# Other PSUM banks for the first tiles of projections, and four moved steps, in a two-block fp32 transformer kernel

## What is computed

```python
# first block
h = rms_norm(x, mix_norm_g); fq, fk, fv, flog, dq, dk, dv = split(h @ w_in)
fox_out  = 8 heads of 64: softmax(q k / 8 + cumulated log forget gates, causal) v
diff_out = 4 heads: rms_norm((softmax(q1 k1 / 8 + alibi) - lam softmax(q2 k2 / 8 + alibi)) v) * (1 - lam_init)
x = x + concat(fox_out, diff_out) @ w_out
h = rms_norm(x, ffn_norm_g); x = x + (silu(h @ w_gate) * (h @ w_up)) @ w_down      # 2816 hidden
x = rms_norm(x, final_norm_g)
# second block
z = rms_norm(x, norm1_g) @ w_in_2 + b_in; q, k, v, c_a, c_b, g_a, g_b = split(z)
br_a = neighbourhood_attention(q, k, v, rpb) @ w_na_out                            # 8 heads
u = depthwise_conv31(c_a * sigmoid(c_b)); br_b = silu(layernorm(u)) @ w_conv_out
x = x + (sigmoid(g_a) * br_a + sigmoid(g_b) * br_b) @ w_out_2
x = x + (gelu(gate) * val) @ w_down_2, (gate, val) = depthwise_conv3(rms_norm(x) @ w_up_2)
return rms_norm(x, norm_f_g)
```

## Time and profile before

| | us |
|---|---|
| median of the runs | 1381.23 |
| lowest and highest | 1380.28, 1381.60 |
| the profiled execution | 1382.35 |
| its span, first to last instruction | 1380.5 |
| TensorE busy in it | 1339.8 |
| VectorE, ScalarE, GpSimd busy | 676.5, 634.0, 665.6 |

### The profile page before, as it was taken

One profiled execution on the slowest core, in us unless ns is written; L12 is line 12 of the kernel. 1 busy time (PEld: TensorE's weight loads), 2 busy tenths in 40 slices (PEclk: granted clock), 3 DMA queues, 4 the chain that ended last, 5 costly groups with the idle time before them and its releaser, 6 DMA issues.

```text
span 1380.5 us, 19366 instructions
## 1 busy us (share of the span) xinstructions
PE 1339.8 (97%) x6540; PEld 1117.4 (81%) x6540; DVE 676.5 (49%) x1219; ACT 634.0 (46%) x998; POOL 665.6 (48%) x884
## 2 busy tenths in 40 slices
PE   7999999899999999999989999999999999999998
PEld 5888987678888888888878878877878888888887
DVE  6588557663222222111687775857345555552111
ACT  5456456754443432333435864454354444442223
POOL 5433243157555554555464224456555545545550
PEclk9999999999999999999999999999999999999999
DMA  5333242123333333333462222323324333333331
GB/s 164 88 77 84 60 120 70 54 76 103 111 91 92 105 99 97 89 96 101 88 148 70 76 78 61 101 82 92 92 80 119 91 93 104 91 91 96 99 96 62
DMA packets 220329, 127.24 MB, mean 92 GB/s; under 512 B 8636, under 2 KB 215881, under 8 KB 220137
## 3 DMA queue, kind: packets, MB, share of 16 engines
q1 hardware_dynamic: 219751, 126.20, 32.5%
q10 hardware_dynamic: 513, 0.21, 0.1%
HBM read 117.56 MB, written 2.47 MB: 87 GB/s over the span
## 4 chain that ended last, share of the span: by engine, by line
PE 90%; DVE 5%; ACT 2%; issue 2%; DMA 0%; ACTq 0%; DVEq 0%
PE PS L748 28%; PE PS L750 28%; PE PS L749 28%; PE PS L937 1%; PE PS L913 1%; PE PS L914 1%; DVE PTL L1926 0%; DMA ROWV<-in_diff_norm_g 0%; PE PS L922 0%; DVE PS L2082 0%; ACTq L1214 0%; ACT XH L1223 0%; PE PS L917 0%; DVE NM L1891 0%; PE PS L806 0%
## 5 line engine op out<-in xcount | busy, mean ns | idle before, releaser
L720 POOL TENSOR_TENSOR WL<-RAW,WH 128x256 fp32r<-128x256 f32 x864 | 659.9, 795 | 683.7 <-ACT WH L1189 680.6
L1189 ACT ACTIVATE WH<-RAW 128x1024 fp32r<-128x1024 f32 (+1 forms) x220 | 228.9, 1043 | 432.5 <-PE PS L750 382.9
L748 PE MATMUL PS<-XH,WH 128*128 128x512 f32 x1072 | 423.7, 395 | 2.6 <-DVE X L1998 1.8
L749 PE MATMUL PS<-XL,WH 128*128 128x512 f32 x1072 | 418.3, 390 | 0.0
L750 PE MATMUL PS<-XH,WL 128*128 128x512 f32 x1072 | 418.3, 390 | 0.0
L748 PEld LDWEIGHTS PS<-XH,WH 128*128 128x128 f32 x1072 | 202.1, 189 | 44.2 <-DVE X L1998 2.6
L750 PEld LDWEIGHTS PS<-XH,WL 128*128 128x128 f32 x1072 | 201.5, 188 | 42.9
L749 PEld LDWEIGHTS PS<-XL,WH 128*128 128x128 f32 x1072 | 201.8, 188 | 39.5 <-issue 0.7
L748 PE MATMUL PS<-HH,WH 128*128 128x512 f32 (+1 forms) x374 | 141.0, 377 | 0.0
L750 PE MATMUL PS<-HH,WL 128*128 128x512 f32 (+1 forms) x374 | 140.9, 377 | 0.0
L749 PE MATMUL PS<-HL,WH 128*128 128x512 f32 (+1 forms) x374 | 140.8, 377 | 0.0
(11 more groups left out here) (332 smaller groups left out, 1920.7 us busy)
## 6 DMA issues: line engine op xcount, KB each, us to landing
RAW<-in_w_up SPq DMA_DIRECT2D x66, 512.0 KB, 3.8
RAW<-in_w_in SPq DMA_DIRECT2D x60, 512.0 KB, 3.9
RAW<-in_w_down SPq DMA_DIRECT2D x32, 512.0 KB, 3.9
RAW<-in_w_gate SPq DMA_DIRECT2D x22, 512.0 KB, 3.8
RAW<-in_w_out SPq DMA_DIRECT2D x16, 512.0 KB, 3.7
RAW<-in_w_down SPq DMA_DIRECT2D x16, 384.0 KB, 3.4
QB<-QA SPq DMA_DIRECT2D x24, 128.0 KB
KA<-KA SPq DMA_DIRECT2D x24, 128.0 KB
```

What stands on the lines that cost most here:

```text
L720: ins = pool.tensor_tensor(WL[:, s, cs], RAW[:, s % 2, cs], WH[:, s, cs].bitcast(F32), ALU.subtract)
L748: pe.matmul(out, ah, bh, start=start, stop=False)
L749: pe.matmul(out, ah, bl, start=False, stop=False)
L1189: act.activation(WH[:, s, 0:width], RAW[:, s % 2, 0:width], ACT.Copy).then_inc(w_hi, 1)
```

## The change

It has five parts.

1. `out_tile_bank`: tiles 0 and 1 of out1, na_out, conv_out and out2 accumulate in TRB, those of ffn1, cab and ffn2 in OB; tiles 2 and 3 of the latter go to ACC. The waits follow: tiles 2 and 3 of all seven now wait for the last two takes of the projection ahead instead of those of tiles 0 and 1.
2. The convolution's early taps: one more behind each of five steps of cab, 5 instead of 2 behind the query take of na0, none behind its key take and the two heads' low parts.
3. In neighbourhood attention the gate tiles start at step 22, not 24, and all eight are in, not six; the late taps start a tile later.
4. In differential attention the key tile of heads 6 and 7 ends at step 20, not 21, head 6 follows it a step sooner, and out1's tiles start at step 21, not 23.
5. SyncE issues a head's bias row ahead of its other two rows.

```diff
         elif kind == "na":
...
-            for c in range(6):
-                s0 = N_SCORES - 8 + 2 * c
-                add("gb", c, TL["gates_b"] + c, UN["gates_b"] + c, s0, min(s0 + 1, N_SCORES + 2))
+            for c in range(KD):
+                s0 = N_SCORES - 10 + 2 * c
+                add("gb", c, TL["gates_b"] + c, UN["gates_b"] + c, s0, min(s0 + 1, LAST_STEP))
         else:
...
-                     ("oa", 1, 14, 14), ("qk", 4, 15, 17), ("qk", 5, 18, 21), ("oa", 2, 23, 25), ("oa", 3, 26, 29),
-                     ("oa", 4, 30, 32), ("oa", 5, 33, 34), ("oa", 6, 35, LAST_STEP), ("oa", 7, LAST_STEP, LAST_STEP)]
+                     ("oa", 1, 14, 14), ("qk", 4, 15, 17), ("qk", 5, 18, 20), ("oa", 2, 21, 23), ("oa", 3, 24, 26),
+                     ("oa", 4, 27, 30), ("oa", 5, 31, 34), ("oa", 6, 35, LAST_STEP), ("oa", 7, LAST_STEP, LAST_STEP)]
...
     def early_bank(s):
 
-        return (ACC, ACC + 1, OB, OB + 1)[s]
+        return (OB, OB + 1, ACC, ACC + 1)[s]
+
+    def out_tile_bank(name, c):
+
+        return TRB + c if c < 2 else ACC + (TL[name] + c) % 2
...
             e, mem = head % 2, FAM[kind]["mem"]
             nat, oth = half_rows(e), half_rows(1 - e)
+            if kind == "diff" or (kind == "fox" and head >= 2):
+                sp.wait_ge(sc_ready, FAM[kind]["s0"] + 4 * (head - 1))
+                dst, src = bias_rows_of(kind, head)
+                sp.dma_start(dst, src).then_inc(head_in[e], 16)
             sp.wait_ge(head_hi, 2 * (FAM[kind]["h0"] + head) + 2)
...
-            if kind == "diff" or (kind == "fox" and head >= 2):
-                dst, src = bias_rows_of(kind, head)
-                sp.dma_start(dst, src).then_inc(head_in[e], 16)
...
-        def first_pair(u, a, bh, bl, chunk_ready):
-
-            for s in range(2):
-                need_acc(a + s)
+        def first_pair(u, bank, bh, bl, chunk_ready):
+
             pe.wait_ge(w_lo, u + 2)
...
                 if c == 0:
-                    need_acc(a)
-                    need_acc(a + 1)
+                    if name == "conv_out":
+                        pe.wait_ge(acc_free, TL["na_out"] + 2)
...
                     for h in range(2):
-                        need_acc(a + h)
+                        need_acc(a + h if c > 2 else TL[name] + h)
...
-            first_pair(UN[name], TL[name], XH, XL, low(base))
+            first_pair(UN[name], OB, XH, XL, low(base))
...
         attention("na")
-        for c in range(6, KD):
-            u = UN["gates_b"] + c
-            fm_tile(u // 4, u % 4, TL["gates_b"] + c)
...
-        first_pair(UN["out2"], TL["out2"], MH2, ML2, low(L0["conv_out"]))
+        pe.wait_ge(acc_free, TL["conv_out"] + 2)
+        first_pair(UN["out2"], TRB, MH2, ML2, low(L0["conv_out"]))
         for c in range(2, KD):
             u = UN["out2"] + c
-            fm_tile(u // 4, u % 4, TL["out2"] + c, MH2, ML2)
+            fm_tile(u // 4, u % 4, TL["out2"] + (c if c > 3 else c - 2), MH2, ML2)
...
             if i >= 2:
-                conv_taps(3, n_early)
+                conv_taps(3 if i < 4 else 4, n_early)
...
             qk_take("na0", i, RP[:, :])
-            conv_taps(2, n_early)
+            if i == 0:
+                conv_taps(5, n_early)
         for i in range(2):
             head_low("na", i)
-            conv_taps(3, n_early)
...
-        for c in range(6, KD):
-            gate_take(c)
-            conv_taps(6)
         for i in range(8):
...
-            if i < 5:
-                conv_taps(6 if i < 4 else len(taps))
-            if i == 4:
+            if i < 6:
+                conv_taps(6 if i < 5 else len(taps))
+            if i == 5:
```

More of the change, by code:

```diff
@@ L543, in program @@
                           24: [("fox", 7)], 30: [("diff", 0)], 32: [("diff", 1)]},
-                  "diff": {5: [("diff", 2)], 8: [("diff", 3)], 12: [("diff", 4)], 16: [("diff", 5)], 21: [("diff", 6)],
+                  "diff": {5: [("diff", 2)], 8: [("diff", 3)], 12: [("diff", 4)], 16: [("diff", 5)], 20: [("diff", 6)],
                            24: [("diff", 7)]},
@@ L778, in first_pair @@
                 for s in range(2):
-                    ins = fm_chunks((u + s) // 4, (u + s) % 4, s, 0, [k], bh, bl, k == 0, k == KD - 1)
+                    ins = fm_chunks((u + s) // 4, (u + s) % 4, bank - ACC + s, 0, [k], bh, bl, k == 0, k == KD - 1)
                     if k == KD - 1:
@@ L1046, in half_units @@
                         for h in range(2):
-                            ins = fm_chunks(u // 4, u % 4, h, k0, [k], bh, bl, k == 0, k == 3, 256, P * h)
+                            ins = fm_chunks(u // 4, u % 4, out_tile_bank(name, h) - ACC, k0, [k], bh, bl, k == 0, k == 3,
+                                            256, P * h)
                             if k == 3:
@@ L1086, in _ @@
         down("down1", L0["ffn1"])
-        first_pair(UN["cab"], TL["cab"], XH, XL, low(L0["down1"]))
+        first_pair(UN["cab"], OB, XH, XL, low(L0["down1"]))
         norm_sum(32, 0)
@@ L1473, in _ @@
         attention("na")
-        for c in range(6, KD):
-            gate_part(c)
-            hi_next(UN["gates_b"] + c)
+        hi_next(UN["gates_b"] + KD - 1)
         for c in range(KD):
@@ L1997, in residual @@
                     tile_ready(name, c)
-                    dve.tensor_tensor(X[:, c, :], ps(TL[name] + c), X[:, c, :], ALU.add).then_inc(acc_free, 1)
+                    dve.tensor_tensor(X[:, c, :], PS[:, out_tile_bank(name, c), :], X[:, c, :], ALU.add).then_inc(acc_free, 1)
                 if c:
@@ L2150, in na_out_take @@
                 dve.wait_ge(act_done, H0["na_out"])
-            dve.tensor_tensor(SG[:, c, :], ps(TL["na_out"] + c), SG[:, c, :], ALU.mult).then_inc(acc_free, 1)
+            dve.tensor_tensor(SG[:, c, :], PS[:, out_tile_bank("na_out", c), :], SG[:, c, :], ALU.mult).then_inc(acc_free, 1)
         dve.wait_ge(ln_ps, 1)
@@ L2185, in _ @@
                     dve.wait_ge(gate_ready, KD)
-                dve.tensor_tensor(tile_t(a), ps(a), SG[:, gate_place(c), :], ALU.mult).then_inc(acc_free, 1)
+                dve.tensor_tensor(tile_t(a), PS[:, out_tile_bank("conv_out", c), :], SG[:, gate_place(c), :],
+                                  ALU.mult).then_inc(acc_free, 1)
                 dve.wait_ge(acc_free, a + 1)
```

## The result

The kernel after takes 1360.76 us (median of 4 runs, 1360.06 to 1360.76), the kernel before 1380.76 (4 runs, 1380.28 to 1381.60; the table ahead of the kernel has the median of three of them, 1381.23): a ratio of 0.9859, 95% interval 0.9848 to 0.9871. The forecast was 1360.7. The profiled execution of after took 1360.75 us with a span of 1358.9, so against the profile of before the span is 21.6 us shorter, 1.6 more than the medians differ, or 1.1 by the earlier median. Some 0.8 of that is an oddity of the one profiled execution of before, as the next table shows.

What follows compares the result with a forecast made beforehand. TensorE, busy 97% of the span, was taken as the bound, so only its waits and clock could move the time. Terms 7.1 + 2.5 + 2.9 + 5.9 + 2.1 = 20.5 us gave 1360.7 us, range 1357 to 1366.5.

Steps and rivals of the forecast that it cites:

- The covers named: Projection entries: ffn2's low part of chunk 7 was done long before need, and na_out's normalisation moves along with TensorE; 7.1 us taken whole.
- The queue: VectorE and ScalarE before v tile 0's take: key take 2.1 us later, take at 720.3, stall shrinking to about 0.6.
- TensorE was free at about 719.83: V projection: TensorE's assumed free time, against a take at 720.3; the stall shrinks to about 0.6, gaining 2.5 us.
- The clock term: V projection, 722.0 to 728.8: a stall of 0.6 us should leave the clock at 2.4 GHz, gaining 2.9 us.
- two terms, 3.4 and 3.0 less 0.5: Neighbourhood attention: step 23's stall filled, 3.4 us; clock kept up, 3.0; less 0.5 showing at step 34; sum 5.9.
- the correction from profile to median: Whole kernel: the median of the runs, 1381.23, lies 1.1 us below the profiled 1382.35, so 1361.9 becomes 1360.7.
- LSUM's cover: Neighbourhood attention's end: two TensorE tiles, 10.9 us, hide VectorE's 9.4 us of taps and sums, with 1.5 to spare.
- Step 24: Differential attention: this step starts 0.6 us sooner, 2.65 less 2.04, once head 6's wait goes.
- worth up to 0.7: Differential attention, steps 24 and 25: VectorE has a take less there, gaining up to 0.7 us.
- then need only the probabilities: Differential attention's last transposes: no longer held until 258.84 by two chunks a step, probabilities done at 258.0, gaining 0.8 us.
- Rival C: Part 4 gives its lower bound and part 1 loses some takes to VectorE's queue: 1364.3 us; chance 0.10.
- what was to show it: Profile signs: named waits gone, v tile 0's take about 0.5 us late, PEclk 1.0, longer last-head wait in out1.

## Why the prediction was right

It was right in sum: 20.0 us against 20.5, and the mechanisms of parts 1, 2 and 3 are there. That the sum came so close is in part luck. Measured alone, parts 1 and 2 gave 0.8 and 0.4 us more than their terms, part 3 and parts 4 and 5 gave 2.0 and 1.1 less, and the order of parts 2 and 3 was the other way.

**Part 1** was 7.1; the traces give 1.7 + 1.1 + 5.5 = 8.3 and the single part 7.9. Each entry lost its printed idle and 0.16, as priced, and another 0.08 by which the start of its second matmul was late. The covers named, ffn2's low parts and na_out's normalisation, held: no wait on them is left.

**Part 2** was 5.4 and was 5.8. The queue was laid out rightly: key take late, ScalarE's rows behind it, the take last. Too small was the stall that was there: the step "TensorE was free at about 719.83" took the WL wait as given, though it lay in front of the same take. Without it, and in the same old time frame, TensorE was free 1.4 us sooner (718.4) and the take done 0.7 sooner (719.6, not 720.3). The clock term, 2.9, was 2.6; that the 1.3 us of stall that are left would not lower the clock was luck as far as its reason goes, since the 2.49 us it was argued from did lower it in two of five profiles.

**Part 3**'s two terms, 3.4 and 3.0 less 0.5, are what the two traces show (5.9; the wait at the end of attention was 0.4 us between starts), and 3.9 is what the part was worth in an ordinary execution. The step that failed is the correction from profile to median: 1.1 us was taken off the whole, when the profiled execution of before stood 1.9 us above the later median, 0.8 by the start of the program and the rest, as far as the traces show, in this place. LSUM's cover held: its matmul in the trace after waits for nothing.

**Part 4** was 2.1 and gave 0.7 in the traces; alone it gave 1.0, which those runs cannot tell from nothing. Three steps failed. Step 24 was 0.2 us sooner, not 0.6, because ScalarE's queue made step 23 wait 1.0. The take that VectorE has less in steps 24 and 25, "worth up to 0.7", and the transposes that "then need only the probabilities" were both wrong, since the transposes wait for VectorE's chain through low parts and probabilities, which the filling does not delay. Rival C, which priced this at its lower bound, was right on part 4 and wrong on part 1.

Of what was to show it, all came but two: the take of v tile 0 came 1.2 us after TensorE was free, not 0.5, and the wait on ML grew by 1.2 (0.4 to 1.6), less than the 2.0 of chunks ahead of it.

## What to carry to other kernels

A stall that ends with an engine's late arrival is worth everything up to that arrival, other waits in front of it included; so price it from when the late engine is done, not from the wait's row. Before terms are read off one profiled execution, look at how far many runs of that kernel lie apart: 15 runs of before spread over 4.5 us, though its first four stayed within 1.3, and some terms were there in some executions only. And moving a weight copy moves the whole ring behind it: the copy that then has to wait blocks what stands behind it in its engine's order, 5.1 us here.

## What the runs showed of the hardware

A stall of 2.9 us in the same place of three kernels was followed by at least 6.2 us at 1.2 GHz, by at least 3.0, or by none. One with 2.48 us printed, in the same place of five profiles, was followed by at least 2.9 us at 1.2 GHz in two of them and by none in three. One of 2.31 us was followed by a fall that came only when TensorE was busy again, and one of 1.84 us was once enough. Whoever counts on "short enough" needs to see the clock in several executions.

A tap of VectorE and a piece of GpSimd's weight work that start 0.02 to 0.03 us apart delayed one another by 0.55 us: the tap in the profile of before, the piece in those of parts 1, 2 and 4. On the critical path that is 0.55 us from one execution to the next. The order of the printed starts did not tell which of them would wait.
